# One unread product behind each attention-score job, others between column sums, the first gates later, the routes turned at half 40

## The reference

```python
# first block, twice (i = 0, 1): each of its three parts has its own shift, scale and gate
mod = silu(c) @ ada_w[i] + ada_b[i]                    # 1024 x 9216
sh0, sc0, g0, sh1, sc1, g1, sh2, sc2, g2 = split(mod, 9)
y = swiglu(x * (1 + sc0) + sh0, w_in, w_out)           # D_FF = 2816
x = layer_norm(DN_ALPHA * x + 0.5 * (1 + g0) * y)
y = retention(h) if i == 0 else nsa(h)                 # second part
x = layer_norm(DN_ALPHA * x + (1 + g1) * y)
# ... and swiglu again, with sh2, sc2, g2

# nsa: 16 heads of 64, 4 groups; three branches, summed under gates
s = q @ k_cmp.T - slopes * dist                        # compressed: 15 keys
s = q @ k_selected.T - slopes * dist                   # selected blocks
s = q @ k_window.T - slopes * dist                     # window
p = masked_softmax(s); o = p @ v

# second block: an even mix (convolution, gated linear attention), peer_ffn, fox_mix, peer_ffn
logits = q @ k.T * scale + c_q - c_k; probs = softmax(causal(logits)); o = probs @ v   # fox, 16 heads
# peer_ffn: top-k of keys picks experts for each token, with softmax gates
act = gelu(h . u[expert]); out = sum(gate * act * v[expert])

# third block: ffn, a mix with causal attention of 8 heads of 64, ffn, final norm
```

## Time and profile before

| | us |
|---|---|
| median of 3 runs | 4168.62 |
| lowest, highest | 4167.13, 4172.46 |
| the profiled execution | 4182.14 |
| its span, first to last instruction | 4180.4 |

### The profile page before, as it was taken

One profiled execution on the slowest core, in us unless ns is written; L12 is line 12 of the kernel. 1 busy time (PEld: TensorE's weight loads), 2 busy tenths in 40 slices (PEclk: granted clock), 3 DMA queues, 4 the chain that ended last, 5 costly groups with the idle time before them and its releaser, 6 DMA issues. The chain is left out here.

```text
span 4180.4 us, 71994 instructions
## 1 busy us (share of the span) xinstructions
PE 3816.2 (91%) x29102; PEld 3451.9 (83%) x29102; DVE 3012.2 (72%) x5922; ACT 1797.2 (43%) x3638; POOL 339.1 (8%) x238
## 2 busy tenths in 40 slices
PE   5999899997899659899999997998999999999698
PEld 4997799996799558899999876698999988897597
DVE  6776777785677485987677965479776787687665
ACT  2444444443444324434444453344444444544243
POOL 0000000000000001850000000057300000000000
PEclk9999999997799859999999997799999999999799
DMA  7757476764166304434444443143444444686243
GB/s 313 265 218 276 153 267 236 265 256 149 66 247 247 140 0 160 153 126 169 171 167 171 157 172 131 52 172 141 152 163 171 169 165 172 223 302 228 93 172 141
DMA packets 118987, 751.73 MB, mean 180 GB/s; under 512 B 13184, under 2 KB 13216, under 8 KB 43008
## 3 DMA queue, kind: packets, MB, share of 16 engines
q1 hardware_dynamic: 117648, 742.97, 48.4%
q10 hardware_dynamic: 688, 3.11, 0.2%
q0 software_dynamic: 320, 1.05, 0.1%
HBM read 744.98 MB, written 1.05 MB: 178 GB/s over the span
## 5 line engine op out<-in xcount | busy, mean ns | idle before, releaser
L909 ACT ACTIVATE weights_high<-weight_ring 128x512 fp32r<-128x512 f32 x2248 | 1294.6, 624 | 1238.9 <-PE bank L193 922.8
L917 DVE TENSOR_TENSOR weights_low<-weight_ring,weights_high 128x512 fp32r<-128x512 f32 x2020 | 1303.9, 690 | 625.9 <-ACT weights_high L909 620.9
L193 PE MATMUL bank<-h_high,weights_high 128*128 128x256 f32 x4800 | 1372.1, 286 | 42.1 <-DVE h_low L667 23.0
L193 PE MATMUL bank<-h_low,weights_high 128*128 128x256 f32 x4800 | 1365.5, 284 | 0.0
L193 PE MATMUL bank<-h_high,weights_low 128*128 128x256 f32 x4800 | 1364.9, 284 | 0.0
L193 PEld LDWEIGHTS bank<-h_high,weights_high 128*128 128x128 f32 x4800 | 927.5, 193 | 61.3 <-issue 40.9
L193 PEld LDWEIGHTS bank<-h_low,weights_high 128*128 128x128 f32 x4800 | 928.1, 193 | 8.6
L193 PEld LDWEIGHTS bank<-h_high,weights_low 128*128 128x128 f32 x4800 | 927.7, 193 | 0.0
L193 PE MATMUL acc<-weights_high,hidden_high 128*128 128x512 f32 x1552 | 613.3, 395 | 0.0
L193 PE MATMUL acc<-weights_low,hidden_high 128*128 128x512 f32 x1552 | 606.4, 391 | 0.0
L193 PE MATMUL acc<-weights_high,hidden_low 128*128 128x512 f32 x1552 | 604.2, 389 | 0.0
(11 more groups left out here) (274 smaller groups left out, 3452.9 us busy)
## 6 DMA issues: line engine op xcount, KB each, us to landing
weight_ring<-stream SPq DMA_DIRECT2D x582, 1024.0 KB, 4.8
h_tok<-slots SPq DMA_DIRECT2D x98, 512.0 KB, 5.7
h_feat<-slots SPq DMA_DIRECT2D x88, 512.0 KB, 5.8
work<-slots SPq DMA_DIRECT2D x30, 512.0 KB, 7.8
mod_sums<-biases SPq DMA_DIRECT2D x8, 1536.0 KB, 9.2
h_feat<-rows SPq DMA_DIRECT2D x8, 512.0 KB, 4.3
work<-biases SPq DMA_DIRECT2D x1, 1536.0 KB, 8.2
x_tok<-x ACTq DMA_DIRECT2D x1, 1024.0 KB, 11.4
```

The costliest lines, as they stand in the source:

```text
L193: ins = self.nc.tensor.matmul(out, lhs, rhs, start=start, stop=stop)
L909: act.activation(k.w_hi[:, b, q * self.QUARTER:(q + 1) * self.QUARTER], self.raw(g, q), ACT.Copy).then_inc(k.highs_ready, 1)
L917: return eng.tensor_tensor(k.w_lo[:, b, w], self.raw(g, q), k.w_hi[:, b, w].bitcast(F32), ALU.subtract)
```

## The change

- Scores: behind each job PE makes one more product, 128x512, from `h_hi` into `acc` bank 3, that nobody reads. It is made in the three NSA branches, in fox and in the third mix.
- Boundaries: `hold_clock` makes unread products of the same shape. With column sums: two ahead of each four column sums, two behind the first eight transposes, four at the end. Without: 13 at the start, two, and four. None in the first boundary. Both gate rows stand behind the transposes, and PE's wait for a free `acc` ahead of the first is gone. These are 8 x 14 + 3 x 19 = 169 products, and 144 in the scores.
- The start: `sums[0]` has two parts (16 slots) and its bias is one row, added into sums that POOL has set to zero; SP waits for POOL. The gates' part, 8 slots, is summed in the first FFN at halves 3 to 15, its gate rows come behind half 25, ACT copies them behind half 26, and PE waits for the copy ahead of half 29. `sums[1]` is carried from half 16 instead of 8. The first load of the ring is 128x168 instead of 128x2048. DVE, ACT and POOL wait for x and the constants ahead of the second stage, no longer ahead of the first.
- Experts: `TURN_AFTER` 39 instead of 35, and DVE's exponentials of the routes (`EXP_AT`) at half 32 instead of 30. The first group of one-hots begins at half 43 instead of 39 and ends where it did.

```diff
     def issue(self, sp, biases, slots, rows):
         k = self.sums.k
         self.host.wait_begun(sp)
-        sp.dma_start(self.sums.where, biases[self.sums.index]).then_inc(k.bias_landed, 16)
+        n = self.sums.parts * D
+        if self.sums.cleared:
+            sp.wait_ge(k.sums_cleared, 1)
+            sp.dma_start(self.sums.where[0:1, :], biases[self.sums.index][0:1, 0:n]).then_inc(k.bias_landed, 16)
+        else:
+            sp.dma_start(self.sums.where, biases[self.sums.index][:, 0:n]).then_inc(k.bias_landed, 16)
...
-        kk, part = self.j // 3, self.j % 3
-        if self.j < 3:
+        parts = self.sums.parts
+        kk, part = self.j // parts, self.j % parts
+        if self.j < parts:
             dve.wait_ge(k.bias_landed, 16 * (self.sums.index + 1))
         else:
-            dve.wait_ge(k.mod_used, self.number - 2)
+            dve.wait_ge(k.mod_used, self.number - parts + 1)
...
+        pool.memset(k.sums[0].where, 0.0).then_inc(k.sums_cleared, 1)
...
+    def hold_clock(self, bank, n):
+
+        k = self.k
+        if self.update is None:
+            return
+        for _ in range(n):
+            k.mm(bank, k.g_hi[:, 0, 0:P], k.g_hi[:, 0:2, :].rearrange("p c t -> p (c t)"), start=True, stop=True,
+                 last=True)
 
     def tensor(self, pe):
         k = self.k
+        if self.sums is None:
+            self.hold_clock(k.bank[:, 2, :], 13)
         if self.sums is not None:
             pe.wait_ge(k.mod_used, self.sums.done)
             for j in range(2 * DC):
+                if j % 4 == 0:
+                    self.hold_clock(k.bank[:, 2, :], 2)
                 mm = k.mm(self.column_sums()[:, j:j + 1], self.sums.where[:, j * P:(j + 1) * P],
                           k.small[:, ONES:ONES + 1], start=True, stop=True, last=True)
             mm.then_inc(k.banks_for_vector.sem, k.banks_for_vector.send())
-            self.wait_acc_free(pe, 0)
-            self.gate_row(pe, 0)
         for t in range(TT):
             if self.norm is not None:
                 pe.wait_ge(k.normed.sem, self.normal + t + 1)
...
                 mm = pe.transpose(self.turned(c, t), self.source(t)[:, c * P:(c + 1) * P], k.c("ident"))
                 if c % 4 == 3:
                     mm.then_inc(k.feature_banks.sem, 1)
-        if self.sums is not None:
-            self.gate_row(pe, 1).then_inc(k.banks_for_scalar.sem, k.banks_for_scalar.send())
+            if t == 0:
+                self.hold_clock(k.bank[:, 2, :], 2)
+        if self.sums is not None and not self.gate_later:
+            for h in range(2):
+                mm = self.gate_row(pe, h)
+            mm.then_inc(k.banks_for_scalar.sem, k.banks_for_scalar.send())
+        self.hold_clock(k.acc[:, 2, :], 4)
...
-        if self.sums is not None:
+        if self.sums is not None and not self.gate_later:
...
+        self.gates_after, self.gates = 25, None
...
+            if self.gates is not None and g == self.gates_after + 4:
+                pe.wait_ge(k.scalar_for_tensor.sem, k.scalar_for_tensor.take())
...
+            if self.gates is not None and g == self.gates_after:
+                pe.wait_ge(k.mod_used, self.gates.done)
+                for h in range(2):
+                    mm = gate_row(k, k.bank[:, 2 + h, :], self.gates.where, h)
+                mm.then_inc(k.banks_for_scalar.sem, k.banks_for_scalar.send())
...
+        if self.gates is not None and g == self.gates_after + 1:
+            act.wait_ge(k.banks_for_scalar.sem, k.banks_for_scalar.take())
+            for h in range(2):
+                ins = copy_gate(k, act, k.bank[:, 2 + h, :], h, 0.5, True)
+            ins.then_inc(k.scalar_for_tensor.sem, k.scalar_for_tensor.send())
...
-    TURN_AFTER = 35
-    EXP_AT = 30
+    TURN_AFTER = 39
+    EXP_AT = 32
...
             product(k.bank[:, i % NB, 0:n]).then_inc(k.banks_for_vector.sem, k.banks_for_vector.send())
+            k.mm(k.acc[:, 3, :], k.h_hi[:, 0, 0:P], k.h_hi[:, 0:2, :].rearrange("p c t -> p (c t)"), start=True,
+                 stop=True, last=True)
...
-        head = Boundary(k, None, False, None, k.sums[0], 0.5, True)
+        head = Boundary(k, None, False, None, k.sums[0], gate_later=True)
...
-    layers.carry(k.sums[n + 1], 24, (0, 1, 2, 3), 8, 64)
+    if (i, j) == (0, 0):
+        layers.gates = k.first_gates
+        layers.carry(k.first_gates, DC, (0, 1, 2, 3), 3, 15)
+    layers.carry(k.sums[n + 1], 24, (0, 1, 2, 3), 16 if (i, j) == (0, 0) else 8, 64)
...
-    k.sums[0].slots(first, 24, range(8), [(0, first.s + 1)] * 24)
+    k.sums[0].slots(first, 2 * DC, range(8), [(0, first.s + 1)] * (2 * DC))
...
-    k.sums = [Sums(k, 0 if n < 6 else DC, k.mod_sums[:, :] if n < 8 else k.work[:, N_WORK - 3 * D:]) for n in range(9)]
+    k.sums = [Sums(k, 0, k.mod_sums[:, 0:2 * D], parts=2, cleared=True)]
+    k.first_gates = Sums(k, 0, k.work[:, N_WORK - D:], parts=1)
+    k.sums += [Sums(k, 0 if n < 6 else DC, k.mod_sums[:, :] if n < 8 else k.work[:, N_WORK - 3 * D:])
+               for n in range(1, 9)]
...
-                    sp.dma_start(k.slot(s), stream[s]).then_inc(k.slot_landed[s % RING], 16)
+                    n = N_COLS if s == 0 else SLOT
+                    sp.dma_start(k.slot(s)[:, 0:n], stream[s][:, 0:n]).then_inc(k.slot_landed[s % RING], 16)
 
         def run(eng, name):
-            eng.wait_ge(k.loaded, 32)
+            if name == "tensor":
+                eng.wait_ge(k.loaded, 32)
             for i, s in enumerate(stages):
+                if i == 1 and name != "tensor":
+                    eng.wait_ge(k.loaded, 32)
```

More of the change, by code:

```diff
@@ L141, in __init__ @@
         self.loaded = ctx.enter_context(nc.semaphore("inputs_loaded"))
+        self.sums_cleared = ctx.enter_context(nc.semaphore("sums_cleared"))
         self.stored = ctx.enter_context(nc.semaphore("output_stored"))
@@ L255, with __init__ @@
 class Sums:
-    def __init__(self, k, c_at, where):
-        self.k, self.c_at, self.where = k, c_at, where
+    def __init__(self, k, c_at, where, parts=3, cleared=False):
+        self.k, self.c_at, self.where, self.parts, self.cleared = k, c_at, where, parts, cleared
         self.index, self.at, self.done = k.n_sums, 0, 0
@@ L472, with __init__ @@
 class Boundary(Inputs):
-    def __init__(self, k, update, gated, norm, sums, gate_scale=1.0, gate_one=False):
+    def __init__(self, k, update, gated, norm, sums, gate_scale=1.0, gate_one=False, gate_later=False):
         super().__init__(k)
         self.update, self.gated, self.norm, self.sums = update, gated, norm, sums
-        self.gate_scale, self.gate_one = gate_scale, gate_one
+        self.gate_scale, self.gate_one, self.gate_later = gate_scale, gate_one, gate_later
         self.layer = update == "layer"
@@ L520, in turned @@
         return self.k.bank[:, 2 * t + c // 4, c % 4 * P:(c % 4 + 1) * P]
[L522 to L527, removed]
     def gate_row(self, pe, h):
         k = self.k
-        return k.mm(k.acc[:, h, :], k.small[:, ONES:ONES + P],
-                    self.sums.where[:, 2 * D + h * BANK:2 * D + (h + 1) * BANK], start=True, stop=True, last=True)
+        return gate_row(k, k.acc[:, h, :], self.sums.where[:, 2 * D:], h)
+    def hold_clock(self, bank, n):
[5 more added lines that the diff above has]
+                 last=True)
     def tensor(self, pe):
         k = self.k
+        if self.sums is None:
+            self.hold_clock(k.bank[:, 2, :], 13)
         if self.sums is not None:
@@ L723, in scalar, with gate_row, copy_gate @@
             self.high(act, 1, t)
-        if self.sums is not None:
+        if self.sums is not None and not self.gate_later:
             act.wait_ge(k.banks_for_scalar.sem, k.banks_for_scalar.take())
             for h in range(2):
-                act.activation(k.gate[:, h * BANK:(h + 1) * BANK], k.acc[:, h, :], ACT.Identity,
-                               scale=self.gate_scale, bias=self.gate_bias())
-    def gate_bias(self):
-        k = self.k
-        if not self.gate_one:
-            return 0.0
-        return k.small[:, BIG:BIG + 1] if self.gate_scale == 0.5 else k.small[:, ONES:ONES + 1]
+                copy_gate(k, act, k.acc[:, h, :], h, self.gate_scale, self.gate_one)
+def gate_row(k, bank, gates, h):
+    return k.mm(bank, k.small[:, ONES:ONES + P], gates[:, h * BANK:(h + 1) * BANK], start=True, stop=True, last=True)
+def copy_gate(k, act, bank, h, scale, one):
+    bias = 0.0
+    if one:
+        bias = k.small[:, BIG:BIG + 1] if scale == 0.5 else k.small[:, ONES:ONES + 1]
+    return act.activation(k.gate[:, h * BANK:(h + 1) * BANK], bank, ACT.Identity, scale=scale, bias=bias)
 class Features(Inputs):
```

12 lines of the change are left out of this document (6 added, 6 removed).

## The result

| | before | changed |
|---|---|---|
| median, us | 4170.5 (4167.1 to 4182.2, 4 runs) | 4310.7 (4298.7 to 4314.0, 4 runs) |
| the profiled execution | 4182.1 | 4298.7 |
| its span | 4180.4 | 4296.6 |
| mean granted clock | 0.936 | 0.928 |

The ratio is 1.032, 95% interval 1.029 to 1.034: slower by 140 us, where +110 was forecast, 4279, with a range of 4168 to 4315; the median lies 4 us inside its upper end. The four executions of either kernel lie within 15 us of each other.

The account below looks back on a forecast made before the run. PE was taken to bound fox, DVE the NSA scores, DVE and DMA the start. Scores +131, boundaries +6 and -3, start -17, turn -7 gave +110: 4168.6 to 4279 us median, range 4168 to 4315.

Parts of the forecast that it names:

- The step that decided: Scores: the granted clock stays at 0.50 despite the added full-array products; with changes of rows paid, chance 0.62.
- Rivals 2 and 3: Scores: clock held at full, products costing only themselves (4114 to 4125, chance 0.18), or changes paid at 0.2 us (4171, 0.08).
- The forecast's row for the selected scores before: NSA selected scores, kernel before: clock 0.50, with PE 6.94 of 7.00 us busy.
- The price of a job: Scores at half clock: 1.38 us with 128 columns, 1.82 with 256, taking 0.25 us for a change of rows.
- Rival 1: Scores: clock low, changes of rows free; +41 in all, 4210 us, chance 0.12.
- +131: All score parts together: NSA selected and window +69, compressed +24, third mix +17, fox +21.
- the compressed branch: NSA compressed scores: 32 jobs of 1.13 us, 36.2 in place of 11.7, +24.
- The net: Eight boundaries with column sums: +0.7 us each, bounds -0.8 to +1.8; +6 together.
- its two terms: Boundaries with sums: unread products' cost less up to 1 us for a held clock; moved gate row returning about half of 1.0.
- The -3 of the boundaries without sums: Three boundaries without column sums: products fill a wait, -1 us each for a clock that doesn't fall, bounds -6 to +1.
- Start: Start: PE begins near 29 us instead of 48.6, -19.5, DMA ending last; net -17, bounds -20 to -11.
- Turn: Experts' turn: half of PE's 6.97 us idle time saved, twice, -3.5 each; -7, bounds -16 to 0.

Follow-up runs that it names:

- four in a row: Kernel before, plus the same 144 unread full-array products, but four in a row behind each fourth score job: 4200.6 us, ratio 1.006.
- three behind each job: Three unread full-array products behind each score job instead of one: two executions only, 4302.2 and 4368.0 us, no median.
- the one pair that ran side by side: Changed kernel without the scores' products: with the later turn 4162.0 us, with turn 35 and exponentials 30 as before 4165.6 us.
- the two pairs: Late against early turn: without the scores' products, 4162.0 and 4165.6 us; without any unread products and fox reordered in fours, 4126.6 and 4129.6 us.

## Why the prediction was right, and where it was off

**The clock.** The step that decided held: 0.50 in all five parts of the scores, from 2 to 5 us behind the begin where a part enters at full. Rivals 2 and 3 fell with the windows of fox. The experiments with four in a row and with three show that they weren't far-fetched: with four in a row the compressed scores ran at 1.00 (1006 to 1017), with three behind each job the selected ones from 1080 on, and with one for each job both at 0.50. The forecast's row for the selected scores before covers their first 7 us; over all 15.8 the clock reads 0.61, but DVE was the bound there, so no term of the sum hangs on it.

**The price of a job.** 0.25 us was taken for a change of rows, from a bound of 0 to 0.28; it is 0.30. The rule of the Trainium skill ("TensorEngine Tiling (Array Packing)", Key Properties), that changing the mode drains TensorE, agrees with this case: 0.29 to 0.30 us for a change at the half clock, and 0.20 at full (fox's first jobs, 0.41 for a product with 0.21 of streaming). Rival 1, free changes, fell with it. The scores came to +137 for +131 by this term and by the compressed branch, where a job took 1.26 us instead of 1.13. By the medians the scores' products cost 147 to 149 us, so the term is short by 16 to 18 there; the traces' parts show 6 of them, and the rest is the matter of the last point below.

**Boundaries.** The net was right (109.2 - 101.8 = +7 for +6), but its two terms were both too small, and that they cancel is luck: the unread products cost 2.0 us in each of the eight, for 1.8 less up to 1 for a held clock, and the gate row behind the transposes returns 1.1, for 0.5. The step that failed is that the clock is held and pays: it was held in two of the eight, and no run shows a gain. The -3 of the boundaries without sums is not there either: the three took 25.8 us for 24.8.

**Start.** -17 for -19.5 at PE's start, and -15 for -17 one stage on. The reason was off: the bound is DVE from the first slot's landing at 9.99. That the two bounds end so near each other, DMA at 29 by the forecast's sum and DVE at 31, is luck.

**Turn.** 3.6 us by the medians of the one pair that ran side by side, for 7; the intervals overlap, so that it is less than 7 is likely and not shown. Its mechanism, a part of the wait coming back as waits for one-hots, is shown: 4 and 6 of 14 us in the two pairs, 9 in the changed kernel, for the half that was forecast. In the traces of the pair the two expert stages are only 1.2 us shorter with the late turn; where the other idle time went stays open.

**The sum against the median.** By the profiled executions the forecast's +110 stands beside +116.5. By the medians it is +140, and the 24 us between are not in the sum's steps: the profiled execution before is 12 us above its median, and that of the changed kernel 12 below. The step that was off is carrying a profile's difference over to the median as if both profiles lay alike. A part of it can be seen. Two kernels with the same work in one stage, the values of the selected branch, show it at different clocks (timeline of PE and windows, first the kernel without the scores' products, then the one with the turn back):

```profile
1049.96 18.28 PE L194 MATMUL bank<-work 128*128 128x64 f32 x96 [0.72 <-ACTq L216]
...
1050.00:1068.20 18.20, 18.20 (x96) 18.05 (x96) 4.88 (x24) 0.00 (x0) 0.00 (x0) 0.57 0.00 1
```

```profile
1047.51 10.93 PE L194 MATMUL bank<-work 128*128 128x64 f32 x96 [0.72 <-ACTq L216]
...
1047.50:1058.40 10.90, 10.89 (x96) 10.79 (x96) 4.88 (x24) 0.00 (x0) 0.00 (x0) 1.00 0.01 2
```

7.3 us hang on where a rise of the clock falls, in one stage of many. The stage was at the slow end in the profile before (18.25 us from 1066.16) and at the fast end in the one after (10.93 from 1112.38). That the rest of the 24 us has the same cause is likely and not shown, since the other runs have no trace.

## What to carry to other kernels

Don't put a product of the full array between products of 64 or 16 rows: it ends the running of two halves at once and pays 0.2 to 0.3 us on each side; if filler is wanted, give it the rows of its neighbours or group it. Look for the same pattern in work that is needed: sorting fox's products by their rows, with no other edit, was worth 19 to 23 us of 4148. And an unread product is only free where PE waits; where PE is the bound or a chain runs through it, count it in full, and give a single profile several us of slack for where the clock rises.

## What was not expected of the hardware

- With 64-row unread products in alternating halves the clock came up in NSA's scores (0.86 over the stretch), while with one full-array product in each 1.45 us job it did not (0.50 over 52 us of the selected branch and 58 of fox, PE busy without a gap).
- At the same number of added columns, 144 products of 64 rows cost 8 us and 144 of 128 rows 149.
- A change of rows costs the same whether it is from 64 to 16, 16 to 64, 64 to 128 or back: 0.29 to 0.30 us at the half clock.
